# One encoder layer on one core: two more block-product rounds in place of half of the fill, convolution norm by streamed squares

## The reference

```
h = rms_norm(x, g_pre_mix)
hc, bg, cg, q, k, v = split(h @ w_in, 6)             # 6 x 512 columns
y_conv = bg * causal_conv3(cg * hc, w_conv)          # depthwise, 3 taps
y_attn = chunked_band_attention(q, k, v, rel_bias)   # 8 heads of 64; 64-row chunks see 8 chunks to the left
y = concat(group_rms_norm(y_conv, g_conv_out, 8), group_rms_norm(y_attn, g_attn_out, 8))
x = x + rms_norm(y @ w_out, g_post_mix)
h = rms_norm(x, g_pre_ffn)
gate, up = split(h @ w_ffn_in, 2)                    # 2816 columns each
x = x + rms_norm((silu(gate) * up) @ w_ffn_out, g_post_ffn)
```

## Time and profile before

| | |
|---|---|
| median of 3 runs | 1108.61 us (1108.59 to 1108.73) |
| profiled execution, its own time | 1108.71 us |
| its span, first to last instruction | 1106.7 us |
| PE busy | 1096.9 us (99%) |
| DVE busy | 759.8 us (69%) |
| ACT busy | 467.3 us (42%) |
| POOL busy | 162.4 us (15%) |
| granted TensorE clock, mean | 0.999 of 2.4 GHz |
| front rounds | 60.8 to 183.9 us |
| attention, with the fill | 183.9 to 367.2 us |

### The profile page before, as it was taken

One profiled execution on the slowest core, in us unless ns is written; L12 is line 12 of the kernel. 1 busy time (PEld: TensorE's weight loads), 2 busy tenths in 40 slices (PEclk: granted clock), 3 DMA queues, 4 the chain that ended last, 5 costly groups with the idle time before them and its releaser, 6 DMA issues.

```text
span 1106.7 us, 15974 instructions
## 1 busy us (share of the span) xinstructions
PE 1096.9 (99%) x5653; PEld 909.5 (82%) x5653; DVE 759.8 (69%) x1206; ACT 467.3 (42%) x818; POOL 162.4 (15%) x258
## 2 busy tenths in 40 slices
PE   9999999999999999999999999999999999999997
PEld 7888888878888888888888888888888888888886
DVE  6878854354546656868787777878787786555584
ACT  6542333555555655734322232323223256444441
POOL 3300022010101220312112211211221110000031
PEclk9999999999999999999999999999999999999999
DMA  7332216300100444535546445543644689776632
GB/s 272 107 120 75 58 57 224 119 20 20 39 3 19 163 162 133 172 95 174 159 142 209 136 122 187 177 146 114 218 136 152 214 307 377 232 237 223 218 114 79
DMA packets 116182, 164.10 MB, mean 148 GB/s; under 512 B 7752, under 2 KB 73304, under 8 KB 116128
## 3 DMA queue, kind: packets, MB, share of 16 engines
q1 hardware_dynamic: 98496, 103.30, 29.3%
q0 software_dynamic: 16464, 55.89, 14.4%
q10 hardware_dynamic: 1168, 4.20, 1.0%
HBM read 119.56 MB, written 46.94 MB: 150 GB/s over the span
## 4 chain that ended last, share of the span: by engine, by line
PE 98%; ACT 1%; DVE 1%; DMA 0%; issue 0%; DVEq 0%; POOL 0%; POOLq 0%
PE psum L1278 34%; PE psum L1305 18%; PE psum L872 12%; PE psum L1111 10%; PE psum L1162 8%; PE psum L1023 4%; PE psum L915 3%; PE psum L896 2%; PE psum L886 2%; PE psum L861 1%; PE psum L999 1%; PE psum L923 0%; PE psum L1005 0%; PE psum L905 0%; ACT arena L1514 0%; PE psum L992 0%
## 5 line engine op out<-in xcount | busy, mean ns | idle before, releaser
L1278 PE MATMUL psum<-arena_r,ws 128*128 128x512 f32 x960 | 224.1, 389 | 0.0
L1278 PEld LDWEIGHTS psum<-arena_r,ws 128*128 128x128 f32 x960 | 180.3, 188 | 37.3
L1278 PE MATMUL psum<-hT,ws 128*128 128x512 f32 x720 | 169.9, 389 | 0.0
L1278 PEld LDWEIGHTS psum<-hT,ws 128*128 128x128 f32 x720 | 135.2, 188 | 27.9
L872 PE MATMUL psum<-hT,ws 128*128 128x512 f32 (+1 forms) x624 | 142.2, 380 | 0.6 <-ACT arena L1540 0.6
L1305 PE MATMUL psum<-hT 128*128 128x512 f32 (+1 forms) x600 | 135.2, 385 | 0.0
L1305 PEld LDWEIGHTS psum<-hT 128*128 128x128 f32 x600 | 111.3, 188 | 22.5
L872 PEld LDWEIGHTS psum<-hT,ws 128*128 128x128 f32 x624 | 107.9, 189 | 19.9 <-issue 0.8
L2408 DVE TENSOR_TENSOR misc<-misc,psum 128x512 f32<-128x512 f32 x100 | 68.6, 686 | 48.3 <-PE psum L1278 46.0
L1729 ACT ACTIVATE ws<-o_raw 128x512 fp32r<-128x512 f32 x40 | 25.1, 627 | 139.1 <-DVE o_raw L2386 138.6
L1162 PE MATMUL psum<-ws,hT 128*128 128x512 f32 x348 | 81.8, 393 | 0.0
(11 more groups left out here) (263 smaller groups left out, 1557.7 us busy)
## 6 DMA issues: line engine op xcount, KB each, us to landing
raw<-in_w_ffn_in SPq DMA_DIRECT2D x44, 512.0 KB, 4.2
act_scratch<-arena POOLq DMA_DIRECT2D x77, 256.0 KB, 3.2
raw<-in_w_in SPq DMA_DIRECT2D x22, 512.0 KB, 3.8
arena<-in_w_ffn_out POOLq DMA_DIRECT2D x22, 512.0 KB, 5.6
arena<-act_scratch SPq DMA_DIRECT2D x38, 256.0 KB, 3.3
arena<-in_x SPq DMA_DIRECT2D x16, 512.0 KB, 6.3
raw<-in_w_out SPq DMA_DIRECT2D x16, 512.0 KB, 3.4
raw<-act_scratch SPq DMA_DIRECT2D x26, 256.0 KB, 3.2
```

Source lines behind the costliest of these rows:

```text
L1278: last = mm(blocks(bank), w[:, k * P:(k + 1) * P], b_operand(i, part, k), start=fresh_bank and k == 0 and w is hi and part == 0, stop=k == ...
```

## The change

The front has eight rounds instead of six: rounds 5, 6 and 7 make q and k of pairs 2, 1 and 0. Those of pairs 2 and 1 are written to DRAM (`store_qk`) and read back. The fill now has 32 pieces, 4 ahead of attention and 28 in it: q and k of pair 3, and the last cg and bg. The norm of convolution blocks 0 to 2 is: ACT squares y and splits the squares (`square_y`, `high_sq`), DVE makes the low part (`low_sq`), PE streams both by a 128x128 matrix of 1/64 in 4 matmuls of 512 columns, so that each channel's row of PSUM holds its group's mean, ACT takes the reciprocal root of 1024 columns (`conv_roots`), and DVE refines it by one Newton step and multiplies (`mix_row`, four chained operations of 1024 columns, of which two read and write PSUM). Block 3 keeps the old way. In attention PE's fill stands between the scores and the transposes instead of behind them, `output` follows the scores, ACT's `read_pT` stands between the two exponentials, and several of DVE's steps move. Loads of the convolution rows move behind `qk_ready` of pair 3. The core of the diff:

```diff
-        act.wait_ge(*((front_out, n) if n else (t_lo, NT)))
+        act.wait_ge(*((t_lo, NT) if n == 0 else (front_out, n) if n < 6 else (c12_made, n)))
...
-    OUT0 = 2 * PAIRS
+    FRONT_PAIRS = 3
+    FILLED = 2 * (PAIRS - FRONT_PAIRS) + 2
+    OUT0 = FILLED
...
-    FRONT = 6
+    FRONT = 5 + FRONT_PAIRS
     RAW0 = FRONT + FIN0 // 2 + PLAIN
     FRONT_ORDER = [(0, 6, 3, 1, 2, 4, 5)] + [tuple(range(OPS))] * (FRONT - 1)
-    SPLIT_ORDER = FRONT_ORDER[:FRONT - 1] + [(0, 1, 2, 3, 4, 6, 5)]
...
-AHEAD = 3
-FILLS = [[1] + [2] * 7 + [1]] * LAST + [[1] + [2] * 4 + [1] * 4]
+AHEAD = 4
+FILLS = [[0, 1, 0, 1, 1, 1, 1, 0, 2], [0, 1, 0, 1, 1, 1, 1, 0, 2], [0, 1, 0, 1, 1, 1, 1, 1, 1], [0, 1, 0, 1, 1, 1, 1, 0, 2]]
...
+    def fill(t, s):
+        for q in range(pieces_ahead(t, s), pieces_ahead(t, s + 1)):
+            piece(q)
     def step(t, s):
         if s == 0:
+            fill(t, s)
             pe.wait_ge(qk_ready, t * 2 + 2)
...
         if scored(t, s):
             if unit(t, s) > 0:
                 pe.wait_ge(biased, unit(t, 2 * s))
             for i in scored(t, s):
                 scores(t, i)
         if s == 0 and t > 0:
-            turn_back(t - 1, NT - 2)
+            output(t - 1, NT - 2)
+        if s == 3 and t == 0:
+            pe.wait_ge(v_back, 64)
+        if s in (3, 5, 7):
+            output(t, s - 3)
         if s == NT and t == LAST:
             pe.wait_ge(biased, PAIRS * UNITS)
             transpose_o(t, PP[1])
...
+        if s == 0:
+            return
+        if s < NT or t < LAST:
+            fill(t, s)
+        pe.wait_ge(exp_done, unit(t, 2 * s))
+        if s > 1:
+            pe.wait_ge(pT_act, tile(t, s - 1))
+        if s == 1 and t == 0:
+            pe.wait_ge(conv_mixed, mixed(LAST - 1))
+        if s == 2 and t > 1:
+            pe.wait_ge(oT_read, t - 1)
+        if s == 1 and t > 0:
+            turn_back(t - 1, NT - 2)
+        transpose_p(t, s - 1)
+        if s == 1 and t > 1:
+            pe.wait_ge(tile_free, tile(t - 1, NT - 2) + 2)
+            transpose_o(t - 1, OT_BANKS)
+        if s == NT and t == LAST:
+            fill(t, s)
             output(t, NT - 2)
...
     def stats(t):
...
+        pe.wait_ge(conv_mixed, means_split(t))
         if t > 0:
...
+            pe.wait_ge(conv_mixed, mixed(t - 1))
+        for half in range(2):
+            for part in (CR, CU):
+                last = mm(PP[2][:, half * HALF:(half + 1) * HALF], same_head, row_r(part)[:, half * HALF:(half + 1) * HALF],
+                          start=(part == CR), stop=(part == CU))
+        last.then_inc(conv_stat, 1)
+    behind = {(4, 2): 0, (5, 0): 1, (5, 5): 2}
     for n in range(FRONT):
         for i in FRONT_ORDER[n]:
             front_multiply(n, i)
             if (n, i) in behind:
-                task, t = behind[n, i]
-                task(t)
+                stats(behind[n, i])
...
+    square_y(0), front_copy_first(4), high_sq(0)
+    front_high(5, 0), conv_roots(0, PP[2]), square_y(1), high_sq(1)
+    for i in range(1, 7):
+        front_high(5, i)
+    conv_roots(1, PP[2]), front_copy_first(5), square_y(2)
+    front_high(6, 0), stage_c11(5), high_sq(2)
+    front_high(6, 1), front_high(6, 2), conv_roots(2, PP[2])
+    for i in range(3, 7):
+        front_high(6, i)
+    for n in range(6, FRONT - 1):
+        front_copy_first(n)
+        for i in range(3):
+            front_high(n + 1, i)
+        stage_c11(n)
+        for i in range(3, 7):
+            front_high(n + 1, i)
+    front_copy_first(FRONT - 1)
...
     def step(t, s):
         more = t < LAST
         if s == 0:
...
+            drain(t, s)
         if more and s == 7:
             high_q(t)
-        read_pT(t, s - 1)
         if s < NT:
             exp(t, 2 * s)
+        if s > 0:
+            drain(t, s)
+            read_pT(t, s - 1)
+        if s < NT:
             exp(t, 2 * s + 1)
-        if s == 1 and t > 0:
-            high_in(2 * t + 1)
+        if not more and s == 7:
+            split_out_a(0)
+        if more and s == 7:
+            high_k(t)
+        if s == 2 and t > 0:
             square_pair(t - 1)
-        if not more and s == 3:
+        if not more and s == 5:
             act.wait_ge(o_var, t)
             squares(t, (0, 1))
...
+        for g in chunks_next(t, s):
+            high_in(g)
         if not more and s == 6:
             split_out_w(0)
...
+        if not more and s == 7:
             split_out_w(1)
-        if not more:
-            squares(t, (4, 5))
+        if not more and s == NT:
+            squares(t, (2, 3, 4, 5))
             split_out_a(1)
             squares(t, (6, 7))
...
+    def low_sq(t):
+        dve.wait_ge(conv_sq, squared(t, 1))
+        tt(row_r(CU), row(CU), row_r(CR).bitcast(F32), ALU.subtract).then_inc(conv_mixed, 1)
+    def mix_row(t):
+        f, mean, y = row(CR), PP[2], row(CONV_ROWS[t])
+        dve.wait_ge(conv_root, t + 1)
+        chain(stt(mean, mean, EPS, f, ALU.add, ALU.mult))
+        chain(stt(mean, mean, -0.5, f, ALU.mult, ALU.mult))
+        chain(stt(f, mean, 1.5, f, ALU.add, ALU.mult))
+        stt(y, y, params[:, t, 3:4], f, ALU.mult, ALU.mult).then_inc(conv_mixed, 1)
...
+    low_sq(0)
     make_u2(4)
     front_low(5, 0)
-    conv_stats_read(0)
     make_u3(4)
-    front_s(5)
-    front_low(5, 1)
-    front_low(5, 2)
+    mix_row(0)
     dve.wait_ge(prod, multiplied(4, 3))
     times(2, 0, BANK[0]).then_inc(c11_done, 1)
-    front_low(5, 3)
     make_c22(4, tiles_of(row(CV), 1), 1)
-    conv_stats_read(1)
-    front_low(5, 4)
+    front_s(5)
+    front_low(5, 1), front_low(5, 2), front_low(5, 3)
     make_c21(4, tiles_of(row(CV), 0), 0)
-    conv_mix(0)
-    front_low(5, 6)
+    low_sq(1)
+    front_low(5, 4), front_low(5, 5)
     make_c12(4)
     times(2, 1, u2).then_inc(front_out, 1)
...
+    front_low(5, 6)
+    for n in range(5, FRONT - 1):
+        q_row, k_row = [row(r) for r in QK_STAGED]
+        make_u2(n)
+        if n == 5:
+            mix_row(1)
+        make_u3(n)
+        front_low(n + 1, 0)
+        if n == 5:
+            dve.wait_ge(conv_stored[1], 16)
+        else:
+            dve.wait_ge(qk_stored, 32 * (n - 5))
+        make_c22(n, tiles_of(k_row, 1), 1)
+        if n == 5:
+            low_sq(2)
+        front_s(n + 1)
+        front_low(n + 1, 1), front_low(n + 1, 2), front_low(n + 1, 3)
+        make_c21(n, tiles_of(k_row, 0), 0)
+        if n == 5:
+            mix_row(2)
+        front_low(n + 1, 4), front_low(n + 1, 5)
+        if n == 5:
+            dve.wait_ge(conv_stored[0], 16)
+        bank_sum(n, 6, tiles_of(q_row, 1), blocks(u2), blocks(BANK[3]), c12_made)
+        front_low(n + 1, 6)
+    n = FRONT - 1
...
+    def drain(t, s):
+        for h in halves_done(t, s):
+            if h // 2 >= CG:
+                read_half(h // 2, h % 2)
+                if h == 2 * CG + 1:
+                    tap(LAST, 0), tap(LAST, 1), tap(LAST, 2)
     def step(t, s):
         more = t < LAST
+        if t == 1 and s == 0:
+            dve.wait_ge(bias_ready, 4)
+        if t == 0 and s == 1:
+            dve.wait_ge(conv_stored[2], 16)
+            dve.wait_ge(qk_stored, 32 * (FRONT_PAIRS - 1))
+        if s == NT and more:
+            low_k(t)
         if s == 0:
...
+            drain(t, s)
         if s < NT:
             add_bias(t, 2 * s)
             add_bias(t, 2 * s + 1)
+        if 0 < s < NT:
+            drain(t, s)
+        if s == 0 and t > 0:
+            copy_o(t - 1, NT - 2)
+        if s in (3, 5, 7):
+            copy_o(t, s - 3)
+        if s == NT and not more:
+            o_finish(t, PP[1])
         if s > 4:
             read_pT(t, s - 1)
...
+        if s == 1 and t > 0:
+            read_o(t - 1, NT - 2)
         if s == 1 and t > 1:
             o_finish(t - 1, OT_BANKS)
...
+        if s == 3 and t > 0:
+            sum_squares(t)
             o_norm(t)
-        if more and s == 4:
-            low_in(2 * t + 2)
-        if more and s == 7:
+        if s == 4:
+            if t > 0:
+                o_scale(t)
+            read_o(t, 0)
+        if s in (5, 7):
+            read_o(t, s - 3)
+        if s == 7 and more:
             low_q(t)
...
+        if s == 7 and not more:
+            split_out_a(0)
             low(OUT0 + 1, out_slot(0), 0)
+        for g in chunks_next(t, s):
+            low_in(g)
...
```

More of the change, by code:

```diff
@@ L595, in _, with next_front @@
             store_v(3, 2, v_stored[1]), store_v(5, 2, v_stored[1]), store_v(7, 1, v_stored[1])
-            for n in range(1, FRONT):
+            def next_front(n):
                 for slot in range(2):
@@ L609, in _ @@
             load_v(0), load_v(1), load_v(2)
-            load_conv(0)
+            sp.wait_ge(qk_stored, 32 * (FRONT_PAIRS - 1))
             load_v(3)
-            load_conv(1), load_conv(2)
-            for t in range(1, PAIRS):
-                for n, at in enumerate((o_q, o_k) if t < LAST else (o_cg, o_bg)):
-                    g, m = 2 * t + n, t + 1 if t < LAST else LAST
-                    free(g)
```

(62 more changed lines are left out.)

217 lines of the change are left out of this document (101 added, 116 removed).

## The result

The changed kernel takes **1123.46 us** (median of 4 runs, 1122.27 to 1123.87) against 1108.62 (4 runs, 1108.59 to 1108.73): ratio 1.0132, 95% interval 1.0114 to 1.0149. It is slower by 14.8 us. The forecast was 1124.0.

A forecast was written before the change was run, and what follows sets the result against it. The prediction took PE's work as the bound while PE stays dense: 1108.7 - 10.7 of PE work + 3.7 front waits + 22.3 attention waits = 1124.0 us, range 1112 to 1130.

The forecast's parts named there:

- PE's work: Whole kernel: two more front rounds +38.3, fill -44.1, norm -7.65 and +2.7, together -10.7 us.
- the prediction's own signs of being wrong: Attention: wrong if PE's waits are below 10 us, matmuls take another time, or the roots' table costs more than its load.
- The front's waits: Rounds 5 and 6: PE waits 1.0 before the second stats, 0.45 before the third, 2.2 before product 3; +3.7 us.
- The disputed price: DVE's mix_row operations in the front: 1.28 us each taken; at 1.8 when writing PSUM, front waits would be +9.6.
- The table load: ACT's load for the roots: 1.28 us, +1.3 if before the first root, 0 before the first exponential; left in the range.
- Attention's waits: 36 attention steps laid out: 25.5 us of PE waits against 3.2 laid out before, so +22.3.
- the bound of 0.1 less a hand-over: Attention: 0.1 us off every hand-over between engines gives +18.6 of new waits; adding it gives +23.7.
- The clock: Rival, chance 0.13: PE's clock drops to 1.2 GHz behind the 3.8 us wait, +2 to +6, so 1126 to 1130.
- Without the taps 3.4 less: Pair 2, step 7: without the three taps ahead of copy_o(4), the layout gives 3.4 us less.
- Without the splits 4.2 less: Attention: without the two chunk splits at their place, the layout gives 4.2 us less.
- The cover holds: Rival, chance 0.10: all new waits stay below 10.7 us and the kernel is faster; 1098.0 with the waits of before.
- half of the waits: Rival, chance 0.07: the 26.0 us of new waits in front and attention are 13, which gives 1111.

The follow-up runs named there:

- gaps filled: The changed kernel with 46 idle transposes put on PE in its two longest attention gaps (30 and 16), no wait removed: 1120.41 us.
- other steps: The changed kernel with the same 28 pieces at other steps: 1111.28 us; the second such kernel also has the third mix_row in round 6: 1109.23 us.
- seven rounds: Against the changed kernel, q and k of pair 2 back in the fill (7 rounds, 48 pieces), low_sq(1) earlier, another table of steps: 1113.80 us.
- taps later: The changed kernel with the three convolution taps moved from pair 2, step 7, to steps 1 and 2 of pair 3: 1120.81 us.
- all three together: The changed kernel with the 28 pieces at yet another table of steps, the third mix_row in round 6 and low_sq(1) earlier: 1107.46 us.

## Why the prediction was right, point by point

**The sign and the mechanism** held. Time falls with PE's work only while PE stays dense; the fill was cover, and where 32 pieces went the waits came: 17.6 us in attention.

**PE's work** in the front: +34.9 with 2.4 of waits in it is 32.5, where the forecast's terms give 38.3 - 7.65 + 2.7 = 33.3. In attention PE's records fell by 38.7, not 44.1. Here one of the prediction's own signs of being wrong came up: matmuls did take another time in the thinner stage. 3.3 of the 5.4 us is the clock (143.3 against 140.0 with the gaps filled). The other 2.1 is there at a clock of 1.00 as well. Counting from the start of each group to the start of the next, less waits, in the kernel with filled gaps, the pieces save some 48 us and not 44.1, but the transposes, the `turn_back`s and the scores, of the same number as before, take 5 us more (the transposes of p 29.2 for 26.1). Why a group takes longer when PE waits behind it is not shown.

**The front's waits**: 3.7 forecast, 2.4 measured. Of the three places the second `stats` has 0.7 (forecast 1.0), the third none (0.45), round 6's product 1.7 (2.2). The disputed price, a DVE operation of 1024 columns that writes to PSUM, came out just below the value taken: 1.23 us where 1.28 was taken, and 1.27 to the next start where 1.31 was. A whole `mix_row` takes 5.0 us for 5.2, which is 0.5 of the 1.3 us for the two that stand in round 5; the rest I did not trace. The lines of the profile grouped by form (count, busy, mean ns):

```profile
L2122 DVE SCALAR_TENSOR_TENSOR arena<-arena,params 128x1024 f32<-128x1024 f32 x3 | 3.9, 1285 | 0.1
...
L2119 DVE SCALAR_TENSOR_TENSOR psum<-psum,arena 128x1024 f32<-128x1024 f32 x3 | 3.7, 1232 | 1.1 <-ACT arena L1549 1.0
L2120 DVE SCALAR_TENSOR_TENSOR psum<-psum,arena 128x1024 f32<-128x1024 f32 x3 | 3.7, 1232 | 0.1
```

The releaser was named as ACT's copy behind `make_c12(5)`; the table of waits names a low part, L2066. The timeline has both:

```profile
184.86 1.28 DVE L2122 SCALAR_TENSOR_TENSOR arena<-arena,params 128x1024 f32<-128x1024 f32 x1
...
187.26 0.68 DVE L2071 TENSOR_TENSOR arena<-misc,psum 128x512 f32<-128x512 f32 x1
...
187.98 0.69 DVE L2066 TENSOR_TENSOR ws<-misc,ws 128x512 fp32r<-128x512 f32 x1
188.04 0.60 ACT L1512 ACTIVATE misc<-psum 128x512 f32<-128x512 f32 x1 [6.77 <-DVE arena L2071]
...
188.78 3.00 PE L1184 MATMUL psum<-hT,ws 128*128 128x512 f32 x12 [1.71 <-DVE ws L2066]
```

The copy ends at 188.64, the low part at 188.67. A table by releaser shows the last one only; both stand behind the last operation of `mix_row`, and both come earlier without it.

**The table load** was put at 0 and in the range. It comes before the first root, and hides:

```profile
143.76 1.28 ACT L1549 ACT_TABLE_LOAD   x1
...
146.19 1.12 ACT L1549 ACTIVATE arena<-psum,eps_col 128x1024 f32<-128x1024 f32 x1 [1.15 <-PE psum L1196]
```

The load ends at 145.04, and ACT then waits 1.15 us more for the sums. The 2.7 us by the Trainium skill ("ScalarE: Activation LUTs", What ACT_TABLE_LOAD costs) is not to be seen here either: no wait of PE stands in that round. The second load, ahead of the first exponential, shows its price plainly:

```profile
224.46 0.60 ACT L1642 ACTIVATE arena<-psum 128x512 f32<-128x512 f32 x1 [4.01 <-PE psum L935]
225.07 1.28 ACT L1616 ACT_TABLE_LOAD   x1
226.37 0.40 ACT L1616 ACTIVATE misc<-misc,nmax 128x128 f32<-128x128 f32 x1
```

The copy ends at 225.06, the exponential starts at 226.37: 1.31 us for the switch, less than half of those 2.7, and the measurement decides. PE waits for ACT in attention for the first time at 266.7, so this one is hidden too. No run takes a load away.

**Attention's waits**: the layout gave 25.5, the trace 18.9 at 18 places. The largest places are the forecast's and of its size: 3.85 for 3.8 (taps), 2.37 for 2.55 (pair 1 to 2), 1.68 for 2.1 (pair 0, step 7). The others were too long, by 6.1 us together, 0.4 for each of the other 15 places. The claim of 20 to 26 us of waits was wrong by this; the bound of 0.1 less a hand-over, worked out as +18.6, was nearer than the value taken, +22.3.

**The clock** was a rival, at 0.13, priced 2 to 6. It did happen, twice, at 3 us in all by the medians (2.2 in the profiled execution), and one fall was behind a wait that I had not counted as long enough. That is the lower end of its price. It had no part in the sum. That the forecast stands within a microsecond of the result is therefore partly errors that cancel: 1124.0 - 4.7 (attention's waits) - 1.3 (the front's) - 0.8 (the front's work) + 3.3 (records at the slow clock) + 2.1 (the other change of records) = 1122.6, against 1122.27 of the profiled execution. That the sum is this close is luck: in attention the waits and the records were off by 4.7 and 5.4 us, in opposite directions. The sign and the places and lengths of the three longest waits are not. The Trainium skill ("TensorE: Matmul & The Clock Gate", HAM oscillation) has idle gaps returning the engine to the low clock; the rows at 295 us and at 334 us agree.

**Without the taps 3.4 less**: measured 2.65, and less than half of it by the waits themselves. The remainder was taken as if nothing else were late behind it and the taps were free elsewhere; the run shows waits of 3.4 us more, at the old place and in the last pair. **Without the splits 4.2 less**: 3.7 of waits, 6.3 in time.

**Transfers**: the load of v was allowed at most 1 us; PE waits 0.7 for it, once.

**The cover holds, half of the waits** (1098 to 1111) did not happen with this table of steps. With other steps it is the half that happens, at 1111.3 and 12.5 us of new waits: it was not a property of the change but of the table.

## What to carry to other kernels

Count filler work twice, as work and as cover: taking out 44 us of it for 38 us of other work returned 18 us as waits and 3 us as slower clock, though two of the three engines were half idle. Before giving up on such a change, lay the remaining filler out against the hand-overs again; the same 28 pieces at other steps were worth 12 us, and the queue order of one DVE operation another 2. Where runs of a kernel scatter by more than its neighbours do, look at the granted clock behind its longest PE waits first; shortening one of these can give more than its own length (here 3.7 us of waits less gave 6.3).

## What the runs showed of the hardware

The granted TensorE clock fell from 2.4 to 1.2 GHz in or behind single PE waits of an otherwise busy stage. With the wait of 3.85 us it fell in all five profiles that have it, with that of 2.4 us in four of five, and with one of 2.56 us. A fall cost 1.5 us (changed kernel, first gap) and 1.6 (seven rounds), but only 0.6 where later waits took up the difference (changed kernel, second gap). It is not the same in each run: of one kernel four runs took 1113.5 to 1113.9 at a mean clock of 0.997 and one 1112.1 at 1.000. In attention no profile has a fall at a wait of up to 1.9 us (the longest of these is in the kernel with the taps later). Where no wait in attention was above 1.3 us (the two kernels with other steps, and all three together) attention ran at 1.00 and the scatter was 0.4 to 0.8 us.

46 transposes without a use, put into the two gaps, kept the granted clock at 1.00 and made the kernel 3.05 us faster.

A DVE operation of 128x1024 with one operand and its result in PSUM takes 1.23 us, no more than the 1.28 of one with operands and result in SBUF.

A load of an activation table between a copy and an exponential took 1.31 us of ACT from the end of the one to the start of the other (1.28 of it the load).

A table by releaser names the last of several; here two were 0.03 us apart.
